# Padding rows out of the later gathers and scatters, the first later expert block written out, two loads moved in an encoder layer with a hierarchical MoE

## The reference

```
h = rms_norm(x); u, v, q, k, va, gate_a, gate_b = split(h @ w_in)
ya = spatial gating of gelu(u), rms_norm(gelu(v)) in chunks of 128, @ w_proj_a
yb = attention in a window of +-128 (8 query heads, 2 key heads, rms norm and
     rotation of q and k, a sink logit per head), @ w_proj_b
x  = x + (sigmoid(gate_a)*ya + sigmoid(gate_b)*yb) @ w_out
h2 = rms_norm(x)
group  = argmax of 4 group logits;  2 best of the group's 8 experts; gates
slots: assignments (1536*2) sorted by expert, each expert padded to blocks of 128
for each block of 128 slots, with its expert e:
    yb = (silu(xb @ w_gate[e]) * (xb @ w_up[e])) @ w_down[e]
y[slot_tok] += yb * slot_w          # a padding slot has token T and weight 0
out = x + y[:T]
```

## Time and profile before

| what | us |
|---|---|
| median of 3 runs | 2146.08 |
| lowest and highest | 2141.89, 2154.14 |
| profiled execution, its own time | 2152.06 |
| its span, first to last instruction | 2150.2 |
| busy: PE, DVE, ACT, POOL | 2092.8, 1303.7, 1073.8, 511.6 |
| mixers and routing (by the PE's lines) | about 0 to 1427 |
| expert loop and its end | about 1427 to 2150 |

### The profile page before, as it was taken

How to read it: one execution, slowest core, us unless ns; L and a number is a source line. 1 busy time by engine, 2 the same in 40 slices (tenths; PEclk the granted TensorE clock), 3 DMA queues, 4 the chain that set the end, 5 groups by cost and what they waited for, 6 DMA issues and landing times.

```text
span 2150.2 us, 30216 instructions
## 1 busy us (share of the span) xinstructions
PE 2092.8 (97%) x10268; PEld 1730.2 (80%) x10268; DVE 1303.7 (61%) x1645; ACT 1073.8 (50%) x1582; POOL 511.6 (24%) x653
## 2 busy tenths in 40 slices
PE   8999999999999999999999999989999999999997
PEld 7788888888788888897888888757788788878886
DVE  5654233465555233555643434458899999899994
ACT  4453333343442332344523232137787788778884
POOL 4251011220541011213500012113212234332221
PEclk9999999999999999999999999999999999999999
DMA  7213222433213323452122225579999998997973
GB/s 229 92 40 98 88 87 92 173 130 108 74 40 108 98 79 98 163 171 69 40 85 82 81 96 205 206 271 357 386 395 394 394 340 299 392 384 262 325 260 88
DMA packets 108657, 396.72 MB, mean 184 GB/s; under 512 B 9282, under 2 KB 15603, under 8 KB 82964
## 3 DMA queue, kind: packets, MB, share of 16 engines
q1 hardware_dynamic: 91812, 335.64, 42.0%
q0 software_dynamic: 16752, 59.83, 10.5%
HBM read 402.78 MB, written 34.60 MB: 203 GB/s over the span
## 4 chain that ended last, share of the span: by engine, by line
PE 42%; DMA 10%; DVE 2%; issue 2%; ACT 2%; SPq 0%; POOL 0%; POOLq 0%; ACTq 0%; DVEq 0%
DMA held_wu<-w_up_e 5%; PE main L512 3%; PE main L514 3%; PE main L513 3%; DMA y<-e_yo,e_prv 2%; PE main L500 2%; PE main L502 2%; PE main L501 2%; PE main L1988 2%; PE main L1990 2%; PE main L1989 2%; DMA e_xg<-h2s,e_nxt 2%; PE main L1976 2%; PE main L1975 2%; PE main L1974 2%
## 5 line engine op out<-in xcount | busy, mean ns | idle before, releaser
L959 DVE TENSOR_TENSOR w_lo<-raw,w_hi 128x1024 fp32r<-128x1024 f32 (+1 forms) x216 | 250.3, 1180 | 320.3 <-ACT w_hi L705 320.2
L705 ACT ACTIVATE w_hi<-raw 128x1024 fp32r<-128x1024 f32 (+1 forms) x216 | 211.7, 1006 | 141.9 <-PE main L514 73.9
L512 PE MATMUL main<-e_g_hi,w_hi 128*128 128x512 f32 x576 | 237.6, 413 | 0.0
L514 PE MATMUL main<-e_g_hi,w_lo 128*128 128x512 f32 x576 | 226.1, 392 | 0.0
L513 PE MATMUL main<-e_g_lo,w_hi 128*128 128x512 f32 x576 | 225.4, 391 | 0.0
L500 PE MATMUL main<-w_hi,e_g_hi 128*128 128x512 f32 (+1 forms) x560 | 203.6, 364 | 2.3 <-DVE e_g_lo L973 2.3
L502 PE MATMUL main<-w_hi,e_g_lo 128*128 128x512 f32 (+1 forms) x560 | 200.2, 357 | 0.0
L501 PE MATMUL main<-w_lo,e_g_hi 128*128 128x512 f32 (+1 forms) x560 | 200.0, 357 | 0.0
L2097 DVE TENSOR_TENSOR e_d_lo<-held_wd,e_d_hi 128x2048 fp32r<-128x2048 f32 x76 | 173.1, 2288 | 36.2 <-ACT e_d_hi L2034 36.1
L2097 DVE TENSOR_TENSOR e_u_lo<-held_wu,e_u_hi 128x2048 fp32r<-128x2048 f32 x76 | 173.7, 2285 | 25.6 <-ACT e_u_hi L2034 25.6
L2097 DVE TENSOR_TENSOR e_g_lo<-held_wg,e_g_hi 128x2048 fp32r<-128x2048 f32 x76 | 173.5, 2283 | 2.5 <-ACT e_g_hi L2034 2.4
(11 more groups left out here) (349 smaller groups left out, 4786.5 us busy)
## 6 DMA issues: line engine op xcount, KB each, us to landing
held_wg<-w_gate_e SPq DMA_DIRECT2D x78, 1024.0 KB
held_wu<-w_up_e SPq DMA_DIRECT2D x78, 1024.0 KB
held_wd<-w_down_e SPq DMA_DIRECT2D x76, 1024.0 KB
raw<-w_in SPq DMA_DIRECT2D x120, 512.0 KB, 3.6
raw<-w_proj_b SPq DMA_DIRECT2D x24, 512.0 KB, 3.6
raw<-w_proj_a SPq DMA_DIRECT2D x24, 512.0 KB, 3.6
raw<-w_out SPq DMA_DIRECT2D x24, 512.0 KB, 4.2
raw<-w_in SPq DMA_DIRECT2D x24, 256.0 KB, 4.6
```

What stands on the lines that cost most here:

```text
L512: pe.matmul(bank[:], hi[:, k, :], mov_hi[:, k, :], start=(k == 0), stop=False)
L514: mm = pe.matmul(bank[:], lo[:, k, :], mov_hi[:, k, :], start=False, stop=(k == KT - 1))
L705: act.activation(hi, buf, ACT.Copy).then_inc(w_hi_done, 1)
L959: dve.tensor_tensor(lo, buf, hi.bitcast(F32), ALU.subtract).then_inc(w_split, 1)
```

## The change

- Padding slots get row numbers from T + 128 (`ROWS`) upward in place of 1024 upward, in `slots` alone; the gathers and scatters of `experts` get a bound, `ROWS - 1`, and leave out the rows beyond it. A row of `xg` that is left out keeps what it held. The two early experts' gathers and scatters are as before.
- PE, ACT and DVE do the part of block 0 and block 1 up to the loop in another order: after gate(1), down(0) comes before up(1); ACT and DVE split the down weights of block 0 and finish its hidden tile before they split the up weights of block 1. The loop on these three starts at 2. SP's and POOL's programs keep their order.
- POOL issues the eight DMAs of the rotation tables in group 1 behind the 32 `weigh` units; its wait for the rotated q goes.
- ACT has in groups 1 and 2 an additional `Exp` of one element a partition at the last q tile of panel PQ + 1, ahead of that tile's squares.

```diff
+ROWS = T + P
...
+                    if g and p == PQ + 1 and j == 3:
+                        act.activation(unread[:, g - 1:g], nsink[:, 0:1], ACT.Exp)
...
+            for s in range(NU):
+                weigh(g, s)
             if g == 1:
-                pool.wait_ge(q_roped, 8 * g + 8)
                 tables(4, 4, "k")
                 tables(4, 4, "q")
-            for s in range(NU):
-                weigh(g, s)
...
-        link(dve.tensor_scalar(pad_id, ids[:, 0:1], float(PADS), None, ALU.add))
+        link(dve.tensor_scalar(pad_id, ids[:, 0:1], float(ROWS), None, ALU.add))
...
-        link(dve.tensor_scalar(value, value, float(-PADS), None, ALU.add))
+        link(dve.tensor_scalar(value, value, float(-ROWS), None, ALU.add))
...
         turn_hidden(0)
+        gate_up(1, "g")
+        down(0)
+        gate_up(1, "u")
+        turn_x(2)
+        turn_hidden(1)
         m = blocks(pe)
-        with pe.Fori(1, m + 1) as i:
+        with pe.Fori(2, m + 1) as i:
...
-            if not first(i):
-                weigh(i - 1)
+            weigh(i - 1)
...
-        body(0)
+        split_hi(1, "g", 0)
+        tanh(0)
+        split_hi(1, "g", 1)
+        x_hi(1)
+        split_hi(0, "d", 0)
+        split_hi(0, "d", 1)
+        hidden_hi(0)
+        split_hi(1, "u", 0)
+        split_hi(1, "u", 1)
+        body(1)
         m = blocks(act)
-        with act.Fori(1, m + 1) as i:
+        with act.Fori(2, m + 1) as i:
...
-        body(0)
+        split_lo(1, "g", 0)
+        glu_gate(0)
+        split_lo(1, "g", 1)
+        glu_up(0)
+        x_lo(1)
+        split_lo(0, "d", 0)
+        split_lo(0, "d", 1)
+        hidden_lo(0)
+        split_lo(1, "u", 0)
+        split_lo(1, "u", 1)
+        body(1)
         m = blocks(dve)
-        with dve.Fori(1, m + 1) as i:
+        with dve.Fori(2, m + 1) as i:
...
-            pool.indirect_dma_start(xg, None, a["h2s"], bass.IndirectOffsetOnAxis(ap=nxt[:, 0:1].bitcast(I32), axis=0)).then_inc(x_in, 16)
+            pool.indirect_dma_start(xg, None, a["h2s"], bass.IndirectOffsetOnAxis(ap=nxt[:, 0:1].bitcast(I32), axis=0),
+                                    bounds_check=ROWS - 1, oob_is_err=False).then_inc(x_in, 16)
...
-                                    compute_op=ALU.add).then_inc(y_out, 16)
+                                    bounds_check=ROWS - 1, oob_is_err=False, compute_op=ALU.add).then_inc(y_out, 16)
```

More of the change, by code:

```diff
@@ L214, in mixers @@
     sink, nsink = place("sink", [P, NH]), place("nsink", [P, NH])
-    half, minus = place("half", [P, 16]), place("minus", [P, 1])
+    half, minus, unread = place("half", [P, 16]), place("minus", [P, 1]), place("unread", [P, 2])
     ssx, rsx = place("ssx", [P, 8]), place("rsx", [P, 8])
```

## The result

The changed kernel takes 2137.8 us in the median of 11 runs (2133.0 to 2143.2), the kernel before 2147.6 us beside it (11 runs, 2141.7 to 2161.7): ratio 0.9943, 95% interval 0.9924 to 0.9963 (the two medians alone give 0.46%). That is faster by 0.57%, about the 0.5% that can be told from no change; the interval reaches down to 0.37%. The forecast was 2122 us with a range of 2113 to 2136; the time lies above both. The profiled execution took 2138.0 us, 14.1 less than that of before.

What follows compares the result with a forecast made beforehand. TensorE, busy for 97% of the span, was taken as the bound, so only its waits and low clock could be won. 6.1 + 6.6 + 14 + 0.7 = 27.4 us off 2152.06 gave 2124.7, adjusted to 2122; range 2113 to 2136.

Steps and rivals of the forecast that it cites:

- Mixers, 6.1 us: Second and third groups' attention: moving rotation table loads and exp's table load removes PE waits and a low clock, 6.1 us.
- The 1.4 us left for the masked scores: Second group's attention: PE wait for masked scores assumed to remain, 1.4 us as in the third group.
- Written-out block, 6.6 us: Start of the later experts: block 0's wait falls from 7.53 to about 1.1 us, block 1's mark 6.6 us sooner.
- Rows left out, 14 us: Expert loop: leaving out padding rows relieves DMA so PE bounds again; 14 of the remaining 15.4 us gained.
- the first term: Expert loop where weights are new: DMA time for a block's 6.29 MB of weights, taken as 15.1 us.
- The second term: Expert loop where weights are new: a block's gathers and scatters, 4.0 us, cut to 4.0 x 0.58 by omitted rows.
- The second effect: POOL in the expert loop: scatters land sooner, so the next gather starts on the transposes alone; inside the 14 us.
- Tail, 0.7 us: End of the span: the last scatter, with 82 of 128 rows in its block, saves 0.7 us, bounds 0 and 2.
- The 6 us between the profiled execution of before and its median: Whole kernel: 2152.06 us profiled against 2146.08 median, unexplained; taking part of it moved the forecast from 2124.7 to 2122.
- B: Expert loop: rows left out relieve nothing, as descriptors still pass or landing is queueing alone; 2133.4 us, chance 0.14.
- C: Start of the later experts: written-out block gains nothing, DVE and PE waits only move; 2129 us, chance 0.12.
- D: POOL in the expert loop: gather and scatter issues get longer, kernel slower, 2185 us or up to 226 us over; chance 0.04.

Runs made afterwards that it cites:

- e9: The changed kernel without its part on rows, and POOL issues the next gather before waiting for the last scatter to land: 2133.9 us, ratio 0.9920.
- e8: The changed kernel without its part on rows, so written-out block and moved loads alone: 2135.2 us, ratio 0.9932.
- e3: The kernel before with the first later block written out alone: 2142.7 us, ratio 0.9985.
- e4: The kernel before with the two moves in the mixers alone (rotation tables' loads, exp's table): 2140.5 us, ratio 0.9978.
- e5: The changed kernel with every row number of the later blocks beyond the bound, so no rows gathered or scattered there: 2119.0 us, one run, beside 2149.5 before.
- e2: The kernel before with the bound and the new padding row numbers alone: 2148.6 us, ratio 1.0025.
- e10: e9 with block 2 of the later experts written out too: 2136.4 us, ratio 0.9945.
- e6: The changed kernel with the bound on the gathers alone, scatters writing padding rows to spare rows: 2136.7 us, ratio 0.9938.
- e7: The changed kernel with the bound on the scatters alone, gathers reading spare rows for the padding: 2135.9 us, ratio 0.9936.
- e1: The changed kernel with rank r of a block on partition (r % 16) * 8 + r // 16 in place of r: 2134.3 us, ratio 0.9943.

## Why the prediction was wrong, point by point

- **Mixers, 6.1 us: right.** The mean of the ten traces with the moves comes to the experts 7.3 us sooner than that of the three without; the profiled pair says 8.2, of which 6.8 are there when ACT loads Gelu's table in the third group (1130.7 for 1137.5), and the rest comes in the routing, where no edit was made. The wait for POOL is gone, the clock stays at 1.00, and the eight issues behind the attention (now 633.16 to 637.5) meet nobody. The 1.4 us left for the masked scores are 1.7. By the 1.38 us of draining that the Trainium skill ("ScalarE: Activation LUTs", "What ACT_TABLE_LOAD costs") adds to each load, the moves would have given, by estimate, up to 8.9 us. The trace does not show it: the load at 541.07 takes 1.28 us, and 1.31 us lie between the end of the instruction before it and the start of the one behind it.
- **Written-out block, 6.6 us: right in mechanism and about right in size.** Block 0's wait fell from 7.53 to 1.54 us (said: 1.1). Block 1's mark came 5.7 us sooner, counted from x (said: 6.6). Block 2's up weights took 8.5 us from issue to use, 7.0 were assumed, so the new wait at block 1's mark is 4.2 and not 3. The term left one thing out: after that wait the clock fell to 0.50, and the interval to block 2 took 20.53 us, 2.8 over. Down to block 36, 3.0 to 5.7 us remain (e9, e8 and e3 against e4, one trace each). By the runs e3 gives 0.15% (interval 0.01% to 0.30%), 3 us.
- **Rows left out, 14 us: the failed step.** "If a row left out costs the engines nothing: 15.1 + 4.0 x 0.58 = 17.4 us" is its sentence, and two things in it are wrong. First, it takes the mean of the 16 engines for the one that is late. The rows that stay lie on about half of the engines, as many on each as before; a scatter of 38 to 57 rows takes 4.8 us as one of 128 did, and the parts of half a weight load land 7.9 us apart in place of 1.0. For the engines that keep their rows the sum stays near 15.1 + 4.0 = 19.1 us a block (an estimate from the earlier trace rows), over the PE's 17.72. Second, the first term was not constant in the mean either: 16.5 us for 15.1, because the packets of left-out rows still pass and some of the weights' packets beside them take over 600 ns. The second term was right in the mean, 2.15 us a block for 2.3. In the mean the two add up to 18.6 us for 17.4. How the loss in time divides between the two stays open, but e5, which has the second in full and not the first, loses nothing from block 4 on.
- **What the 14 us could have been.** The forecast booked 14 of the 15.4 us that the loop lost behind its first interval. With no row left at all (e5) the 36 intervals still lose 5.2 us; e8, without a bound, loses 14.5. All rows together are thus worth 9.3 us in the loop, in one trace each. The 16 to 19 us that e5's one run lies under e8 and the change hold also 4.8 us behind block 36's mark, where its last scatter has nothing to move. The second effect, scatters that land sooner, is not there for the change: 10.9 us to landing in the busy stretch, 10.5 over the span against 10.3. Measured, the part gives 0 to -5 us: alone it is slower by 0.25% (e2), and the change without it is no slower (e8, e9).
- **Tail, 0.7 us: nothing.** The last scatter's issue stands 7.55 us before the end of the span, 7.66 before.
- **The 6 us between the profiled execution of before and its median.** The former has a late gather that costs 5.3 us. Whether the other runs of before lacked it can't be seen, as they have no trace; the two traces of the change show that it is not free of such stalls, so they were not a gain to be booked.

Of the rivals, B had it in part in its condition (the descriptors still pass) and nearly in its time, 2133.4 us for 2137.8 measured (12.7 us of gain; 0.57% are 12.2); none had the uneven engines. B's chance of 0.14 was far too low, since it needed only one fact that no row of the trace before could show. C's claim that the waits only move fails for the change, where 3.0 to 5.7 of 6.6 us stay, and holds for the second block written out in e10. D didn't come: gathers take 1436 ns on the average to issue, 1422 before. That DVE's hold on a shared port makes an issue long was not put to a test in any run.

**Left open.** Why a packet of 4 bytes lengthens packets of 8192 of another queue by 100 ns and more, and whether it is the number of these packets or that they may all go to one place; no run parts the two. Which partitions' rows go over which engine, since the record does not name it. And how much of the change's lateness is the longer packets: it loses 7.5 and 9.1 us in blocks 4 to 16 with its engines busy for 94% of the stretch in the mean, e8 6.6 us with them busy for all of it. The uneven engines explain that 94% lose as much as 100%, not the difference of the two. The Trainium skill ("DMA: Bandwidth & Descriptors", "Why small descriptors are slow (HBM only)") puts a small descriptor's cost at some three cycles and 32 bytes of metadata; by that, an estimate, each would be nearly free, and the 108 to 196 ns measured here are not.

## What to carry to other kernels

Before a DMA saving is multiplied by a mean share, ask which of the 16 engines it relieves: a load waits for its last part, so bytes that go from half of the engines may give nothing. The distance between the first and the last landing of a load (1.0 us before, 7.9 in the change), and the number of packets in flight, show it. An indirect transfer with a bound also drops the bytes of a row and not its packet: in these kernels 15 of the 23 us that the rows saved came back in the packets of the other queue, so look at its us per MB as well as at the shrinking one's. In a stretch that the DMA paces, an order written out at its start wins once and does not add up; find the mark where the gain is counted (here block 16), before writing out the next block. Where one trace shows stalls that other executions of the kernel may lack, a forecast should not book them as a gain against a median of other runs.

## What the runs showed of the hardware

- Left-out rows of indirect transfers: 4 bytes a packet in gathers, 8 in scatters with an add (e6, e7), 9 ns each by their own record, and 0.3% to 5.2% of the 8192-byte packets of the other queue over 600 ns, in step with the number of small packets.
- Scatters of 38 to 57 rows out of 128 have 7 to 11 row packets in flight and take 4.8 us, those of 128 rows 14 to 20 and 4.8 us. Placing rank r on partition (r % 16) * 8 + r // 16 leaves this as it is (7 to 11, 4.2 us; e1).
- The 16 parts of half a weight load land 1.0 us apart before, 2.1 in e8, 7.9 with the bound and 2.0 with all rows left out (e5).
- TensorE's clock fell to 0.50 for four microseconds after a wait of 4.20 us at 1462.5, and not after the one of 1.54 us at 1440.1; in the earlier trace rows it fell after 4.5 and 7.53 us.
- The same gather takes 0.99 to 1.05 us to issue in most blocks and 6.73 us at 1936.23. The rise is again in a late start, and the two scatter issues behind such late gathers took 3.04 and 3.11 us in place of 1.6. Other scatter issues, with no such gather before them, took up to 5.95 us before and 5.67 us after.
